# The latent-query stage of a hybrid decode step moved into the joint stage, with paged attention loading its queries per sequence

## What is computed

```python
scale = (MLA_NOPE + MLA_ROPE) ** -0.5          # 64 + 32
q_lat = jnp.einsum('bthn,chn->bthc', q_nope, w_uk)           # 64 -> 256 latent channels
s_past = (jnp.einsum('bthc,bkc->bhtk', q_lat, past_lat)
          + jnp.einsum('bthr,bkr->bhtk', q_pe, past_pe))
...
p = jax.nn.softmax(jnp.concatenate([s_past, s_new], axis=-1) * scale, axis=-1).astype(c_kv.dtype)
o_lat = (jnp.einsum('bhtk,bkc->bthc', p[..., :P], past_lat)
         + jnp.einsum('bhtk,bkc->bthc', p[..., P:], c_kv))
return jnp.einsum('bthc,chv->bthv', o_lat, w_uv).reshape(B, T, H * MLA_V)
```

## Time and profile before

| | us |
|---|---|
| median of 3 executions | 2646.86 (2646.4 to 2649.51) |
| the profiled execution | 2648.35 |
| its span | 2646.6 |
| TensorE busy in it | 2468.6 (93%) |
| VectorE, ScalarE, GpSimd busy | 1455.8, 1071.2, 581.1 |
| mean granted TensorE clock | 0.961 of full |

### The profile page before, as it was taken

How to read it: one execution, slowest core, us unless ns; L and a number is a source line. 1 busy time by engine, 2 the same in 40 slices (tenths; PEclk the granted TensorE clock), 3 DMA queues, 4 the chain that set the end, 5 groups by cost and what they waited for, 6 DMA issues and landing times. The chain is left out here.

```text
span 2646.6 us, 43029 instructions
## 1 busy us (share of the span) xinstructions
PE 2468.6 (93%) x15406; PEld 2199.3 (83%) x15406; DVE 1455.8 (55%) x2596; ACT 1071.2 (40%) x2351; POOL 581.1 (22%) x447
## 2 busy tenths in 40 slices
PE   6999999999999999999969999669999996899998
PEld 6999987788887888788858888569999995799987
DVE  3345543355533654355538888458888884334332
ACT  3233431234312443133326666248888883111111
POOL 0023212123101330033204555431000000222322
PEclk9999999999999999999969999679999997899999
DMA  6678776777776876567553342073334403565651
GB/s 184 191 191 221 203 211 168 205 208 218 206 225 183 230 214 196 150 169 197 168 184 100 127 135 73 26 174 98 83 88 109 115 20 107 175 163 166 168 167 53
DMA packets 489444, 414.69 MB, mean 157 GB/s; under 512 B 52177, under 2 KB 440402, under 8 KB 482066
## 3 DMA queue, kind: packets, MB, share of 16 engines
q1 hardware_dynamic: 469314, 390.71, 52.7%
q10 hardware_dynamic: 18768, 17.04, 2.1%
q0 software_dynamic: 1152, 4.19, 0.5%
HBM read 306.14 MB, written 143.44 MB: 170 GB/s over the span
## 5 line engine op out<-in xcount | busy, mean ns | idle before, releaser
L66 PE MATMUL a_bank<-a_h_hi,a_w_hi 128*128 128x512 f32 (+3 forms) x1680 | 606.6, 361 | 21.7 <-DVE a_w_lo L755 16.4
L68 PE MATMUL a_bank<-a_h_hi,a_w_lo 128*128 128x512 f32 (+3 forms) x1680 | 595.0, 354 | 0.0
L67 PE MATMUL a_bank<-a_h_lo,a_w_hi 128*128 128x512 f32 (+3 forms) x1680 | 594.7, 354 | 0.0
L66 PEld LDWEIGHTS a_bank<-a_h_hi,a_w_hi 128*128 128x128 f32 (+1 forms) x1680 | 314.7, 187 | 68.6 <-DVE a_w_lo L755 20.0
L572 ACT ACTIVATE a_w_hi<-a_w_raw 128x1024 fp32r<-128x1024 f32 x168 | 174.9, 1042 | 436.9 <-PE a_bank L68 297.2
L68 PEld LDWEIGHTS a_bank<-a_h_hi,a_w_lo 128*128 128x128 f32 (+1 forms) x1680 | 314.4, 187 | 43.8
L67 PEld LDWEIGHTS a_bank<-a_h_lo,a_w_hi 128*128 128x128 f32 (+1 forms) x1680 | 314.9, 187 | 38.5
L755 DVE TENSOR_TENSOR a_w_lo<-a_w_raw,a_w_hi 128x1024 fp32r<-128x1024 f32 x168 | 204.2, 1216 | 206.1 <-ACT a_w_hi L572 206.0
L1783 ACT ACTIVATE t_prob<-t_bank,t_nm 128x512 f32<-128x512 f32 (+3 forms) x320 | 195.4, 620 | 41.0 <-DVE t_nm L1844 40.5
L1837 DVE TENSOR_REDUCE t_mx<-t_bank 128x1 f32<-128x512 f32 (+3 forms) x320 | 185.9, 604 | 45.1 <-PE t_bank L1895 32.3
L1827 DVE TENSOR_TENSOR t_pt<-t_bank,t_pt 128x512 fp32r<-128x512 f32 (+3 forms) x320 | 188.2, 605 | 27.9 <-ACT t_pt L1769 25.0
(11 more groups left out here) (322 smaller groups left out, 5183.1 us busy)
## 6 DMA issues: line engine op xcount, KB each, us to landing
a_w_raw<-in_w_in SPq DMA_DIRECT2D x164, 512.0 KB, 4.5
between_zT<-a_zo SPq DMA_DIRECT2D x164, 256.0 KB, 3.8
between_LAT<-in_lat_pool SPq DMA_DIRECT2D x256, 128.0 KB, 2.6
p_lat<-between_LAT SPq DMA_DIRECT2D x64, 512.0 KB, 3.1
y_mg<-between_zT SPq DMA_DIRECT2D x112, 128.0 KB, 2.6
t_qt<-between_QT SPq DMA_DIRECT2D x16, 768.0 KB, 13.0
a_x<-in_x_prompt SPq DMA_DIRECT2D x16, 512.0 KB, 5.4
m_zt<-between_zT SPq DMA_DIRECT2D x16, 512.0 KB, 4.8
```

Of the source, the lines that this page charges most:

```text
L66: pe.matmul(out, lh, rh, start=start, stop=False)
L67: pe.matmul(out, lh, rl, start=False, stop=False)
L68: return pe.matmul(out, ll, rh, start=False, stop=stop)
```

## The change

The stage `latent_queries` and the tile `qall` are gone. In the joint stage:

- The sample tile (g = 93) also stores the rotary rows of the queries, 16 further transfers: for each of the two parts and each of 8 sequences, 32 rows x 8 heads x 8 tokens from SBUF, so 256 pieces of 32 bytes, into a new DRAM tensor QR.
- In slots 258 to 280, between the tiles 12 and 13, w_uk comes in already transposed from the host as `w_ukt` (128 rows: two heads of 64), is split (one ScalarE, one VectorE instruction over 128 x 1024), two v tiles are zeroed by GpSimd and filled by 4 transfers with the queries of head pairs in a block-diagonal form, and TensorE does 2 x 4 x 3 matmuls of 128 rows and 128 columns. Their result is split by 2 + 2 instructions over 128 x 512 and stored by 2 transfers to a new DRAM tensor QL.

In paged attention, SP loads QL[b] (one transfer) and QR[b] (four) into `qb[u]` behind the loads of a sequence's first group, GpSimd zeroes the rotary parts of both buffers once, and VectorE's eight copies are gone.

```diff
@@ front
+        LQ = SLOTS * (SEC - 1)
+        LQ_TILE = (SEC - 1) * PER + 1
@@ front, sync, tile(e, k) at k == 7
                         sp.dma_start(dst, src.bitcast(F32)).then_inc(st_q, 16)
+                        if sample:
+                            for b in range(DEC_B):
+                                sp.dma_start(T["QR"][b, :, x].rearrange("r (h t) -> r h t", h=NH),
+                                             src[NOPE:QD, :, b * DEC_T:(b + 1) * DEC_T].bitcast(F32)).then_inc(st_r, 16)
@@ front, sync, loop over g
+                if g == LQ + 6:
+                    done(sp, "rota", LQ_TILE - 1)
+                    sp.dma_start(ukt_raw, T["w_ukt"]).then_inc(lq_in, 16)
+                elif g == LQ + 14:
+                    sp.wait_ge(lq_nil, 2)
+                    sp.wait_ge(st_q, 32 * LQ_TILE)
+                    for x in range(2):
+                        for e in range(2):
+                            pairs = T["QS"][x, 0:NOPE].rearrange("d (a e) t -> d e a t", e=2)
+                            sp.dma_start(qz[x][NOPE * e:NOPE * e + NOPE, :, e].bitcast(F32), pairs[:, e]).then_inc(lq_q, 16)
+                elif g == LQ + 28:
+                    sp.wait_ge(lq_ol, KC)
+                    for c in range(KC):
+                        sp.dma_start(T["QL"][:, :, c].rearrange("b p n -> p b n"), ql[c][:].bitcast(F32)).then_inc(lq_st, 16)
...
@@ front, gpsimd
+                if g == LQ + 8:
+                    done(g_, "o", LQ_TILE - 1)
+                    for x in (v_hi, v_lo):
+                        g_.memset(x[:].bitcast(F32), 0.0).then_inc(lq_nil, 1)
@@ front, scalar
+                if g == LQ + 14:
+                    a.wait_ge(lq_in, 16)
+                    done(a, "o", LQ_TILE - 1)
+                    a.activation(ukt_hi, ukt_raw, ACT.Copy).then_inc(lq_hi, 1)
+                for c in range(KC):
+                    if g == LQ + 22 + 2 * c:
+                        a.wait_ge(lq_made, KC)
+                        a.wait_ge(st_q, 32 * LQ_TILE)
+                        a.activation(ql[c][:, :, 0:NS].rearrange("p b (h t) -> p h b t", h=NH),
+                                     bk[:, B0 + c].rearrange("p (h b t) -> p h b t", h=NH, b=DEC_B), ACT.Copy).then_inc(lq_oh, 1)
@@ front, vector
+                if g == LQ + 15:
+                    v.wait_ge(lq_hi, 1)
+                    v.tensor_tensor(ukt_lo, ukt_raw, ukt_hi.bitcast(F32), ALU.subtract).then_inc(lq_lo, 1)
+                for c in range(KC):
+                    if g == LQ + 23 + 2 * c:
+                        v.wait_ge(lq_oh, c + 1)
+                        v.tensor_tensor(ql[c][:, :, NS:2 * NS].rearrange("p b (h t) -> p h b t", h=NH),
...
@@ front, tensor
+                if g == LQ + 20:
+                    p.wait_ge(lq_lo, 1)
+                    p.wait_ge(lq_q, 64)
+                    for x in ("knl", "amk", "rog", "osq", "oe"):
+                        done(p, x, LQ_TILE - 1)
+                    for c in range(KC):
+                        for x in range(NH // 2):
+                            w = slice(c * P, (c + 1) * P)
+                            rh, rl = (t[:, x].rearrange("p e t -> p (e t)") for t in qz)
+                            i = three(p, bk[:, B0 + c, x * P:(x + 1) * P], ukt_hi[:, x, w], ukt_lo[:, x, w], rh, rl, True, True)
+                        i.then_inc(lq_made, 1)
-def latent_queries(nc, T, qall):
...
@@ attend_paged, sync
+            def queries(b, u):
+                if b >= 2:
+                    grp(sp, "qk", b - 2, NG)
+                else:
+                    sp.wait_ge(q_nil, b + 1)
+                sp.dma_start(qb[u][:, 0:2].bitcast(F32), T["QL"][b]).then_inc(q_in[u], 16)
+                for k in range(G):
+                    sp.dma_start(qb[u][ROPE * k:ROPE * k + ROPE, 2 + k].bitcast(F32), T["QR"][b].rearrange("r x n -> r (x n)")).then_inc(q_in[u], 16)
+
             def load(b, u):
                 for j in range(NG):
+                    if j == 1:
+                        queries(b, u)
@@ attend_paged, gpsimd
+            for u in range(2):
+                g.memset(qb[u][:, 2:6].bitcast(F32), 0.0).then_inc(q_nil, 1)
             g.memset(ones[:], 1.0).then_inc(ready, 1)
@@ attend_paged, vector
-            def queries(b, u):
-                grp(v, "qk", b - 2, NG)
-                v.tensor_copy(qb[u][:], qall[:, :, ds(b, 1), :].rearrange("p k b n -> p k (b n)").bitcast(F32)).then_inc(S["qc"], 1)
@@ attend_paged, tensor
-                        seq(p, "qc", x[0])
+                        p.wait_ge(q_in[x[1]], 80 * (x[0] // 2 + 1))
```

More of the change, by code:

```diff
@@ L212, in front @@
         raw = zs[:].rearrange("p a b -> p (a b)")
+        ukt_raw = zs[:].rearrange("p a b -> p (a b)").rearrange("p (a c) -> p a c", c=KL)
+        ukt_hi, ukt_lo = (t[:].rearrange("p a b -> p (a b)").rearrange("p (a c) -> p a c", c=KL) for t in (qk_hi, qk_lo))
+        qz = [t[:].rearrange("p a (e t) -> p a e t", e=2) for t in (v_hi, v_lo)]
+        ql = [qt_hi, qt_lo]
         bk = ps("a_bank", [P, 8, 512])
@@ L226, in front @@
         zin_qk, zin_c, zin_g = (sem("m_zin_" + x) for x in "qk c g".split())
-        st_ro, st_c, st_q, st_k, st_p, st_v, st_s = (sem("m_st_" + x) for x in "ro c q k p v s".split())
+        st_ro, st_c, st_q, st_k, st_p, st_v, st_s, st_r = (sem("m_st_" + x) for x in "ro c q k p v s r".split())
         tabled, gathered = sem("d_tabled"), sem("d_gathered")
+        lq_in, lq_nil, lq_hi, lq_lo, lq_q, lq_made, lq_oh, lq_ol, lq_st = (sem("l_" + x) for x in "in nil hi lo q made oh ol st".split())
         s_in, s_out = ([sem(f"d_{x}{u}") for u in range(2)] for x in ("s_in", "s_out"))
@@ L456, in _ @@
             sp.wait_ge(st_s, 16)
+            sp.wait_ge(st_r, 32 * DEC_B)
+            sp.wait_ge(lq_st, 16 * KC)
         def bc(ap, *shape):
@@ L660, in tile @@
                         a.wait_ge(s_cross, UNITS)
+                        a.wait_ge(st_r, 32 * DEC_B)
+                    if e == LQ_TILE:
+                        a.wait_ge(lq_st, 16 * KC)
                     for x in range(2):
@@ L942, in _ @@
                 each_tile(g, tile)
+                if g == LQ + 15:
[5 more added lines that the diff above has]
+                        v.tensor_tensor(ql[c][:, :, NS:2 * NS].rearrange("p b (h t) -> p h b t", h=NH),
+                                        bk[:, B0 + c].rearrange("p (h b t) -> p h b t", h=NH, b=DEC_B),
+                                        ql[c][:, :, 0:NS].rearrange("p b (h t) -> p h b t", h=NH).bitcast(F32),
+                                        ALU.subtract).then_inc(lq_ol, 1)
                 if r == SLOTS - 1 and s + 1 < SEC:
@@ L1002, in tile @@
                         p.wait_ge(s_whole, 1)
+                    if e == LQ_TILE:
+                        p.wait_ge(lq_ol, KC)
                     for h in range(RH):
@@ L1201, in attend_paged @@
-def attend_paged(nc, T, qall, ol):
+                if g == LQ + 20:
[9 more added lines that the diff above has]
+                        i.then_inc(lq_made, 1)
@@ L1204, in attend_paged @@
+def attend_paged(nc, T, ol):
     G, NG = 4, N_PAGES // 4
@@ L1231, in attend_paged @@
         groups = "qk low sa mxs ex tp pth ptl nh nl pv".split()
-        seqs = "qc red nm den rcp dg of oc rs fin".split()
+        seqs = "red nm den rcp dg of oc rs fin".split()
         halves = "tq lth ltl".split()
@@ L1236, in attend_paged @@
         zin = [[sem(f"p_zin{u}{j}") for j in range(NG + 1)] for u in range(2)]
+        q_in, q_nil = [sem(f"p_q_in{u}") for u in range(2)], sem("p_q_nil")
         consts, ready, masked = sem("p_consts"), sem("p_ready"), sem("p_masked")
@@ L1450, in result @@
                                 ALU.mult).then_inc(S["fin"], 1)
-            queries(0, 0)
             keys_low(0, 0, 0)
@@ L1456, in _ @@
                 if x:
-                    if x[2] == 0:
-                        queries(x[0], x[1])
                     keys_low(*x)
@@ L1625, in decode @@
         ol = sb("ol", [P, 2, NH, NS])
[L1626 to L1629, removed]
+        attend_paged(nc, T, ol)
         latent_values(nc, T, ol)
@@ L2202, in hybrid_step @@
 def hybrid_step(nc, T):
-    for name, shape in (("zT", (N_IN, NT)), ("PE", (2, ROPE, SEQ)), ("QT", (NH, 2, QD, SEQ)), ("QS", (2, QD, NH, NS)),
+    for name, shape in (("zT", (N_IN, NT)), ("PE", (2, ROPE, SEQ)), ("QT", (NH, 2, QD, SEQ)), ("QS", (2, QD, NH, NS)), ("QL", (DEC_B, P, 2, P)), ("QR", (DEC_B, ROPE, 2, NH * DEC_T)),
                         ("KT", (NH, 2, NOPE, SEQ)), ("VS", (SEQ, NH, 2 * VD)), ("ROT", (2, RH * RD, NT)),
@@ L2241 @@
         "w_in": w_in[0], "w_uq": w_uq[0], "w_uk": w_uk.reshape(KL, NH * NOPE), "w_uv": w_uv.reshape(KL, NH * VD),
+        "w_ukt": w_uk.reshape(KL, NH // 2, 2, NOPE).transpose(2, 3, 1, 0).reshape(P, NH // 2, KL),
         "w_ret": w_branch_ret[0], "w_mla": w_branch_mla[0], "w_out": w_out[0],
```

## The result

The changed kernel takes 2635.81 us in the median of 5 executions (2630.18 to 2637.35). The kernel before, measured beside it, takes 2648.91 (2646.4 to 2650.92, 5 executions). The ratio is 0.9946, with a 95% interval of 0.9931 to 0.9961: by the ratio 14 us faster, from 10 to 18 (13 by the two medians). 19.3 us were forecast. A later measurement on one chip agrees: 2635.53 against 2649.34, ratio 0.9942 (0.9923 to 0.9961).

What follows compares the result with a forecast made beforehand. TensorE, busy 2468.6 of 2646.6 us, was taken as the bound, with gains where it stands still or runs at the lower clock. -26.7 + 2.6 + 4 + 0.8 = -19.3 us from 2646.86 gives 2627.6, range 2618 to 2639.8.

Steps and rivals of the forecast that it cites:

- The stage removed: Between joint stage and paged attention: the latent-query stage with one of its two barriers goes, -26.7 us.
- The marks on GpSimd: GpSimd's first instructions of the latent-query stage and paged attention, behind the same barrier: 1359.91 - 1333.21 = 26.70 us.
- The product inside the joint stage: In the joint stage: 24 added matmuls cost TensorE +2.6 us; work added on other engines is hidden.
- The 16 stores: Sample tile, g = 93: stores hold SyncE 10.5 us, less 6.0 absorbed; taken as +4, from 0 to 14.
- 6.0 us for VectorE's updates, which a delay absorbs: Sample tile: SyncE's 6.0 us of waits for VectorE absorb that much of the stores' 10.5, leaving 4.5.
- a lost stretch of 3.4 us: TensorE at a mean clock of 0.57 for 8 us costs 3.4 us, counted only above the stores' +4.
- Paged attention: Start of paged attention: five more SyncE transfers delay the second group's rotary load, +0.8 us, from 0 to 3.
- the -2.2: Paged attention: bound on the gain from removing VectorE's eight copies, from TensorE's 2.2 us of waits; nothing was given.
- Hidden: Rival at g = 93: the 16 stores cost nothing, total -23.3 us, 2623.6; chance 0.26.
- In full: Rival at g = 93: stores cost their whole length and a clock stretch, total -9.3 us, 2637.6; chance 0.18.
- The slower rival: Rival at g = 93: queue takes store issues no faster than it drains, 2.11 us each, +7.9, 2654.8; chance 0.05.
- The gap: Rival before paged attention: the gap stays because something of the joint stage holds its first loads; chance 0.04.

Runs made afterwards that it cites:

- before_qr: The kernel before with only the 16 QR stores added at g = 93, and waits for them: 2659.0 us against 2649.23, ratio 1.0031.
- qr_late: The changed kernel with the 16 QR stores taken out of g = 93 and made as QS-to-QR copies in slots 264 to 279: 2623.72 us, ratio 0.9904.
- late_half: qr_late with 75 semaphore increments on SyncE at g = 93, no transfer: 2630.45 us, ratio 0.9931 to the kernel before.
- late_spdelay: qr_late with 150 semaphore increments on SyncE at g = 93, no transfer: 2635.37 us, ratio 0.9945 to the kernel before.
- late_copies: qr_late with an unused 128 x 768 VectorE copy for each sequence of paged attention again: 2624.45 us against 2623.72 for qr_late.
- late_gather: qr_late without gathers in slots 92 to 109, all later ones following 18 slots later: 2621.78 us, ratio 0.9898 to the kernel before.
- before_gather: The kernel before with only the gathers moved out of slots 92 to 109: 2640.76 us, ratio 0.9962.
- after_gather: The changed kernel, stores still at g = 93, with the gathers moved out of slots 92 to 109: 2615.91 us, ratio 0.9884 to the kernel before.
- gather_mm2: after_gather with each of the 24 new matmuls made twice: 2615.86 us.

## Why the prediction was right, and where its size was off

**The stage removed** (-26.7). From the joint stage's last matmul to paged attention's first transpose the trace gives -26.3. The marks on GpSimd, and leaving SyncE's 1.4 us of increments out, were right.

**The product inside the joint stage** (+2.6). Measured +2.7 between the landmarks around it, 2.63 for the matmuls themselves, and none of the added work on the other engines shows.

**The 16 stores** (+4). This term was mis-sized: +8.0 us in the profiled executions (100.4 against 92.4) and 8 to 12 by the times (before_qr, and the changed kernel over qr_late). The issue price was not the fault: 0.45 us was measured and 0.64 taken, so SyncE lost 7.7 us where I had 10.5. The step that failed is "6.0 us for VectorE's updates, which a delay absorbs". The delay did take up those waits, but while SyncE waited there, its weight load and projection store were draining. Without that pause the state store is issued right behind them and lands later: the waits for landing grew by 6.3 us, as much as the others shrank. That the queue absorbed nothing shows in the start of its last state store, in the kernel before, the changed one, qr_late, late_half and late_spdelay:
```profile
476.32 0.38 SPq L343 DMA_DIRECT2D out_st_s<-m_zs  x1
487.28 0.44 SPq L350 DMA_DIRECT2D out_st_s<-m_zs  x1
476.69 0.38 SPq L350 DMA_DIRECT2D out_st_s<-m_zs  x1
481.51 0.43 SPq L350 DMA_DIRECT2D out_st_s<-m_zs  x1
486.33 0.43 SPq L350 DMA_DIRECT2D out_st_s<-m_zs  x1
```
Counted from the first QS store these are 73.1, 80.9, 73.5, 77.7 and 82.4 us: a delay of 7.7 us comes out as 7.7, one of 4.1 as 4.2 and one of 8.9 as 8.9. With the measured price my rule would have given 7.7 - 6.0 = 1.7 us, further from the 8.0; the price set too high hid part of the fault, and that the term came no further off is luck.

The second half is the clock: I kept a lost stretch of 3.4 us for the upper bound, and every kernel with SyncE delayed in that tile had more of it (20.5 to 23.9 us at the lower level between 400 and 520, against 13.7). TensorE's waits alone grew by 5.3, 1.0 and 5.3 us for the three delays, which looks as if some were absorbed, but the tile grew by 8.0, 5.1 and 10.4. Whether the lower clock took the place of waits or added to the loss, these runs don't separate.

**Paged attention** (+0.8). The second group's transposes wait for the rotary load, as forecast:
```profile
1359.46 0.88 PE L1491 MATMUL p_bank<-p_ident,p_lat 128*128 128x128 f32 x3 [1.20 <-DMA p_pe<-between_PEK]
```
That is 3.36 us after the first, where it was 2.61: 0.75 later. It is made up again: from the first transpose to the next stage's load it is 325.5 us against 326.2, and 326.0 against 326.9 in the mean of all kernels with the new and the old code (nine and three). So the stage came out about 1 us shorter, where I had +0.8 and nothing for VectorE's copies; by late_copies they may be the reason, within the -2.2 that I had as their bound.

**Rivals.** "Hidden" (2623.6) is the time of qr_late, 2623.72, with the stores elsewhere. "In full" (2637.6) is nearest to what happened, in the time and in the mechanism: the whole length of the stores and a clock stretch, at 7.7 us where it had 10.5. The slower rival fell: the stores were issued at 0.45 us, not at over 1.6, and late_spdelay shows their bytes and pieces to cost nothing beside SyncE's time, to within about 1 us. The Trainium skill's 512 B in DMA: Bandwidth & Descriptors, Specifications, may hold for the rate, but it says nothing on the time of such a store alone; here one of 256 pieces of 32 bytes landed in 1.7 us in the median, from the row
```profile
L400 SPq DMA_DIRECT2D between_QR<-m_qt_hi x8: 450/451/717, 406.9 to 410.7; - x8
...
DMA to landing us min/median/max: 1.6/1.7/3.3
```
The gap did not stay.

## What to carry to other kernels

Before work is moved onto a queue that "has waits", ask what drains during those waits: here a pause that let earlier transfers land was not free time, and delays of 4.1, 7.7 and 8.9 us each came out whole at the queue's end. Where a transfer-issuing queue takes as long for its loop as the engine with the most work, look for issues to move out of that stretch, small ones too; here moving 18 gathers into slots with time gave 8.6 us, more than half as much as removing a whole stage (13). A stage border was well priced here from one engine's first instructions behind two barriers (26.7 us forecast, 26.5 and 26.3 measured).

## What was not expected of the hardware

150 semaphore increments on SyncE took 8.9 us and 75 took 4.1, 55 to 59 ns each.

TensorE's clock fell in a stretch in which the trace shows it busy throughout: in the kernel before, 8.00 of 8 us at a mean of 0.57, among the sample tile's matmuls of 8 and 64 columns. The two kernels with free gathers and without the stores (late_gather, before_gather) both kept one stretch of 6.8 us at the lower level and 86.4 us for the tile; the two with the stores (after_gather, gather_mm2) had none and took 83.3 us. Why 8 us of stores earlier in the queue should spare that stretch was not tried and stays open.
